# Opening of a two-block transformer kernel: squares added on VectorE into one tile, one sum on TensorE, and the spreading product two half columns later

## What is computed

```python
m  = (silu(c)     @ w_ada[l] + b_ada[l]).reshape(b, 1, N_MOD, d)      # nine modulation vectors
mc = (silu(c_ctx) @ w_ada[l] + b_ada[l]).reshape(1, 1, N_MOD, d)
x  = x + 0.5 * m[:, :, 2] * swiglu(modulate(rmsnorm(x, norm_ffn1[l]), m[:, :, 0], m[:, :, 1]), w_ffn1_in[l], w_ffn1_out[l])
# rmsnorm: x * rsqrt(mean(x * x) + EPS) * g      modulate: h * (1 + scale) + shift
```

## Time and profile before

| | before |
|---|---|
| median of 3 runs | 1579.8 us (1579.7 to 1580.3) |
| profiled execution, first to last instruction | 1577.3 us |
| TensorE matmul busy | 1418.1 us, 90% |
| VectorE busy | 1121.3 us, 71% |
| ScalarE busy | 618.1 us, 39% |
| GpSimd busy | 403.3 us, 26% |
| DMA | 435.95 MB, mean 276 GB/s |

### The profile page before, as it was taken

How to read it: one execution, slowest core, us unless ns; L and a number is a source line. 1 busy time by engine, 2 the same in 40 slices (tenths; PEclk the granted TensorE clock), 3 DMA queues, 4 the chain that set the end, 5 groups by cost and what they waited for, 6 DMA issues and landing times.

```text
span 1577.3 us, 19688 instructions
## 1 busy us (share of the span) xinstructions
PE 1418.1 (90%) x7237; PEld 1050.6 (67%) x7237; DVE 1121.3 (71%) x2287; ACT 618.1 (39%) x1353; POOL 403.3 (26%) x385
## 2 busy tenths in 40 slices
PE   8899999999999999999999998888887777777777
PEld 6688888889888999999889994333333333333322
DVE  3876775557876687777898778677777666666754
ACT  4222122213566444445565654333333333333322
POOL 0000010001200100011006236544454444444440
PEclk9999999999999999999999999999999998999999
DMA  8754585445642366555545589999999999999996
GB/s 323 272 191 143 167 287 191 159 138 171 209 147 67 121 201 187 170 176 170 160 134 163 197 330 401 420 421 422 422 421 422 420 422 421 421 422 421 422 422 282
DMA packets 86191, 435.95 MB, mean 276 GB/s; under 512 B 9488, under 2 KB 13584, under 8 KB 53072
## 3 DMA queue, kind: packets, MB, share of 16 engines
q0 software_dynamic: 45024, 298.08, 46.9%
q1 hardware_dynamic: 41072, 136.62, 26.8%
HBM read 433.61 MB, written 1.05 MB: 276 GB/s over the span
## 4 chain that ended last, share of the span: by engine, by line
PE 63%; DMA 15%; DVE 15%; ACT 4%; issue 1%; POOL 1%; SPq 0%; ACTq 0%; DVEq 0%; POOLq 0%
PE ps L585 15%; PE ps L586 15%; PE ps L587 15%; PE ps L1005 13%; DMA HF<-in_puv,AB 8%; DMA WF<-in_puv,AB 4%; DMA work<-in_puv,AB 2%; DVE WR L1411 2%; DVE work L2248 1%; PE ps L623 1%; DVE HF L2248 1%; PE ps L764 1%; ACT L1386 1%; DVE ring L2248 1%; ACT WR L1025 1%
## 5 line engine op out<-in xcount | busy, mean ns | idle before, releaser
L585 PE MATMUL ps<-HR,WR 128*128 128x256 f32 (+2 forms) x1224 | 389.1, 318 | 8.5 <-DVE WR L1411 6.9
L586 PE MATMUL ps<-HR,WR 128*128 128x256 f32 (+2 forms) x1224 | 384.4, 314 | 0.0
L587 PE MATMUL ps<-HR,WR 128*128 128x256 f32 (+2 forms) x1224 | 384.4, 314 | 0.0
L1411 DVE TENSOR_TENSOR WR<-ring,WR 128x1024 fp32r<-128x1024 f32 (+1 forms) x245 | 285.6, 1172 | 118.7 <-ACT WR L1025 117.2
L1025 ACT CAST WR<-ring 128x1024 fp32r<-128x1024 f32 (+1 forms) x245 | 241.8, 993 | 291.7 <-PE ps L587 291.6
L585 PEld LDWEIGHTS ps<-HR,WR 128*128 128x128 f32 x1224 | 233.7, 191 | 26.1 <-issue 7.3
L586 PEld LDWEIGHTS ps<-HR,WR 128*128 128x128 f32 x1224 | 233.8, 191 | 14.0 <-issue 0.2
L587 PEld LDWEIGHTS ps<-HR,WR 128*128 128x128 f32 x1224 | 233.6, 191 | 14.0
L585 PE MATMUL ps<-AR,WR 128*128 128x256 f32 (+1 forms) x535 | 165.4, 309 | 0.9 <-DVE AF L1818 0.9
L586 PE MATMUL ps<-AR,WR 128*128 128x256 f32 (+1 forms) x535 | 164.9, 308 | 0.0
L587 PE MATMUL ps<-AR,WR 128*128 128x256 f32 (+1 forms) x535 | 164.9, 308 | 0.0
(11 more groups left out here) (335 smaller groups left out, 2245.3 us busy)
## 6 DMA issues: line engine op xcount, KB each, us to landing
AB<-in_w_adaT POOLq DMA_DIRECT2D x56, 512.0 KB, 4.6
ring<-in_f1i SPq DMA_DIRECT2D x44, 512.0 KB, 4.6
ring<-in_f2i SPq DMA_DIRECT2D x44, 512.0 KB, 3.6
ring<-in_w SPq DMA_DIRECT2D x29, 512.0 KB, 3.5
ring<-in_f1o SPq DMA_DIRECT2D x21, 512.0 KB, 3.9
ring<-in_f2o SPq DMA_DIRECT2D x16, 512.0 KB, 3.6
ring<-in_wq SPq DMA_DIRECT2D x16, 512.0 KB, 4.4
ring<-in_w_ada SPq DMA_DIRECT2D x12, 512.0 KB, 9.1
```

The costliest lines, as they stand in the source:

```text
L585: e.matmul(o, l[0], r[0], start=first, stop=False)
L586: e.matmul(o, l[0], r[1], start=False, stop=False)
L587: return e.matmul(o, l[1], r[0], start=False, stop=last)
L1411: e.tensor_tensor(WS[:, m % NSP, 1, 0:nk * cols], ring[:, ring_of(m) % NS, 0:nk * cols], WS[:, m % NSP, 0, 0:nk * cols].bitcast(F32), ALU. ...
```

## The change

Three tables are written in another order, and VectorE adds more:

- VectorE adds all eight squares into `S(0)`, with seven additions in place of four; each waits for the one before it.
- TensorE makes one sum, 4 products in place of 16.
- In TensorE's order both halves of block 1 and the first half of block 2 stand ahead of the spreading product, with columns 0 and 1; before, it was the first half of block 1 and column 0.
- ScalarE copies out the rows of block 1 (`row_out(1)`) ahead of the root, and no longer behind the shift of block 0.

```diff
-OPEN = [half(0, 0), half(0, 1), ("sum", 0), ("sum", 1), ("sum", 2), ("column", 0), ("sum", 3), half(1, 0), ("spread",), half(1, 1)]
-OPEN += around(2) + around(3) + [("f1", 0, (0, 1)), ("f1", 1, (0, 1))] + around(4)
+OPEN = [half(0, 0), half(0, 1), half(1, 0), ("column", 0), half(1, 1), ("sum",), half(2, 0), ("column", 1), ("spread",), half(2, 1)]
+OPEN += around(3) + [("f1", 0, (0, 1)), ("f1", 1, (0, 1))] + around(4)
...
                 elif s[0] == "sum":
-                    p = s[1]
-                    o = bank("rms", "x") if p == 0 else bank_of("rms", "x")
-                    q.wait_ge(*dv.at("sq", "x", p))
+                    o = bank("rms", "x")
+                    q.wait_ge(*dv.at("sq", "x"))
                     for t_ in range(4):
-                        x = e.matmul(o[:, t_:t_ + 1], S(2 * p)[:, 128 * t_:128 * t_ + 128], K("ones")[:, 0:1],
-                                     start=p == t_ == 0, stop=p == t_ == 3)
-                    if p == 3:
-                        x.then_inc(*mm.to("rms", "x"))
+                        x = e.matmul(o[:, t_:t_ + 1], S(0)[:, 128 * t_:128 * t_ + 128], K("ones")[:, 0:1],
+                                     start=t_ == 0, stop=t_ == 3)
+                    x.then_inc(*mm.to("rms", "x"))
...
             row_out(0)
+            row_out(1)
             root(("x",), small[:, 0:4])
...
             column(0)
-            row_out(1)
             hi(1)
...
-            for p in range(4):
-                q.wait_ge(*ac.at("sq", "x", 2 * p + 1 if p < 3 else 6))
-                if p == 2:
+            for a, b_, last in ((0, 1, 1), (2, 3, 3), (0, 2, 3), (4, 5, 5), (0, 4, 5), (6, 7, 6), (0, 6, 6)):
+                q.wait_ge(*ac.at("sq", "x", last))
+                if b_ == 5:
                     last_square("x", XT[:, 7, :], S(7), (s_x[1], 16))
-                if p == 3:
-                    q.wait_ge(*dv.at("sqlast", "x"))
-                e.tensor_tensor(S(2 * p), S(2 * p), S(2 * p + 1), ALU.add).then_inc(*dv.to("sq", "x", p))
+                q.wait_ge(*dv.now())
+                e.tensor_tensor(S(a), S(a), S(b_), ALU.add).then_inc(*dv.to("sq", "x"))
```

## The result

The change takes 3.8 us off: median 1576.26 us (1575.16 to 1578.35, 12 runs) against 1580.04 us (1578.92 to 1581.54, 12 runs), a ratio of 0.9977 with a 95% interval of 0.9970 to 0.9985. The forecast was 1576.2. The profiled execution took 1573.3 us in place of 1577.3.

The account below looks back on a forecast made before the run. The opening was taken as one chain: TensorE to column 3, VectorE to block 7, a load, TensorE again. 3.9 won less 0.3 given back gives 3.6 us, 1576.2 against 1579.8; 8-in-10 range 1574.6 to 1579.3.

Parts of the forecast that it names:

- The start: TensorE behind block 0, which ends at 11.15 us: idles 2.25 us until block 1's weights land at 13.4.
- The additions: VectorE behind block 7's square: four dependent additions, 4 x 0.73 = 2.92 us, tile ready at 16.99, 0.3 ahead of TensorE.
- The spreading product: TensorE: 0.9 us at the upper clock level, half of 1.80; VectorE goes on at 21.4, 1.8 us earlier.
- Column 2: TensorE waits 1.5 us for ScalarE's copy of block 2's rows, does the column at 26.5; gain set here, 3.9 us.
- Behind it: From column 2 to TensorE's restart: same order, restart at 65.6 in place of 69.50 us, transfers cost nothing.
- Given back: Around TensorE's restart: the clock's rise may not move along with it; 0.3 us lost, bounds 0 to 1.95.
- Rival 1: The clock falls in TensorE's new idle time ahead of block 1; gain 1.2 us, 1578.6 us; chance 0.17.
- Rival 2: A later wait, above all TensorE's 5.49 us ahead of 69.50, takes up the gain; 1579.8 us; chance 0.10.
- Rival 3: Slower: lower clock from 13.4 us to beyond the spreading product, column 2 at 33.2; 1582.6 us; chance 0.04.
- Rival 4: Timed runs before lose two more half products to the clock than the profile; 2 x 0.8 more won, 1574.6; chance 0.09.

Follow-up runs that it names:

- after again: The changed kernel run and profiled once more with nothing altered, on one chip with another run: 1577.26 us, ratio to before 0.9979.

## Why the prediction was right

**The start.** Right. The wait for block 1's weights was 2.34 us (2.25 said); they landed 0.3 us later than in the profile before, an execution's own scatter (13.15 to 13.97 in the profiles here), and what hangs on them is that much later than written.

**The additions.** Right to 0.02: four dependent additions took 2.94 us (2.92 said), and the sum's start, 17.59, is that of TensorE and not of VectorE, whose tile was ready at 17.24. A dependent addition starts 0.73 to 0.80 us behind its predecessor; the two independent ones of before, each 0.69 long and 1.28 together, start 0.6 apart. So a link costs 0.13 us or more, and not the 0.04 of the prediction; its sum came out because it took 0.69, and not 0.6, as the step without dependence. The flush that the Trainium skill names (VectorE: DVE Perf Modes, The DRAIN you can't avoid) would have put the end at about 18.7 by the same start, an estimate; the trace does not agree, since it shows 17.24.

**The spreading product.** Mis-sized by 0.2: 1.08 us from start to start, where I had halved 1.80. With the 0.3 of the later landing VectorE went on at 21.90, 1.3 earlier than before and not 1.8.

**Column 2.** Right: 26.92, behind a wait of 1.56 us for ScalarE (1.5 said), with the gain larger here (3.5) than at the spreading product (1.3). The run with block 2's rows early shows that the wait was ScalarE's order: without it the first mark came 2.03 earlier, 0.4 of it from the landing.

**Behind it.** Right, and the strongest part: the distance from the first feed-forward product to GpSimd's loads is 26.36 us before and 26.35 after. No transfer was late: block 6's weights took 5.8 us to land in place of 7.4, and VectorE took them up at 38.45 without a wait (38.05 said).

**Given back.** The size was met by chance. In the first profile the clock rose at about 71.3 (0.68 over 70 to 72), 5.2 us behind the restart, where it was 4.5 before, and the gain went from 3.43 to 3.05 us: 0.38 lost, 0.3 said. In the second profile of the same kernel it rose at about 69.5 (0.62 over 68 to 70), 3.9 us behind its restart at 65.63, and the gain grew from 3.87 to 4.13. Over all the profiles here the rise lies 3.6 to 6.1 us behind the restart, so the term can have either sign. Behind the opening all do the same work, and yet the gain goes on moving. The table follows four VectorE instructions (lines of the kernel before) through three profiles:

| start, us | before | after | gain | after again | gain |
|---|---|---|---|---|---|
| L1582 | 93.70 | 90.65 | 3.05 | 89.57 | 4.13 |
| L1848 | 534.21 | 530.54 | 3.67 | 531.96 | 2.25 |
| L2134 | 898.36 | 894.70 | 3.66 | 896.91 | 1.45 |
| L2257, first | 1573.33 | 1569.34 | 3.99 | 1572.54 | 0.79 |

One place where the three part is 504 to 520 us, with a mean clock of 0.68, 0.89 and 0.79; another is 438 to 442 us, with 1.00, 1.00 and 0.57. The span of the first profile is 4.0 us shorter and that of the second 0.8, for the same kernel. So the opening's 3.5 us is what the change does, shown at the same two marks in both profiles (3.48 and 3.49; 3.57 and 3.56), and medians over many runs, 3.8 and 3.5 us, average over the rest. That the forecast of 3.6 lies within 0.2 of both is in part luck: the chain won 0.4 less than the 3.9 written, and the 0.3 set against it was not a loss of the change.

**The rivals.** Rival 1, the clock falling in the new wait, exists: eight profiles have this wait unfilled, with 1.15 to 2.37 us, and one of them shows the fall (three have over 2.2 us). There it took 1.6 us at the first mark, less than the 2.7 I had worked out, since the level was back before the second half product of block 1 began. The Trainium skill says (TensorE: Matmul & The Clock Gate, What's actually happening) that activity releases the throttle. The trace agrees: the clock was back at about 17.5 us, when half (1,0) had run. Rival 2, a gain lost at the gap ahead of 69.50, is out: the gap is 5.54 us, and 5.14 in the second profile, and moved with the rest. Rival 3 was not seen in any profile. Rival 4, a larger gain because the timed runs of before lose more than its profile, is not needed: 3.8 measured, 3.6 said. There is no second profile of the kernel before, so where the clock falls in its other executions is not shown.

**What the forecast had not separated.** It added up times along one path and had no shares for the parts. The runs give them, and they are not additive: the fewer products alone, -1.2 us at the first mark; the order alone, -0.8; both, +3.5. Each half of the change by itself still meets the fall of the clock (at 21.7 us in the one run, in the wait ahead of 14.01 in the other); the two together do not. In the kernel before, the higher clock is worth 3.28 us from the third sum on, and 2.25 when it is bought with a filler. The prediction prices the half products at 1.84 for 3.50 us, but says nowhere that this is most of the gain. The "two half columns" of the title are the half products (1,1) and (2,0); the second column ahead of the spreading product is worth -0.2.

## What to carry to other kernels

Fewer instructions on the busiest engine are worth nothing until the engine has other work where they stood: take the products away and move independent products into their place in one step, or neither. Where TensorE's clock falls in a stretch of thin products and waits, look at the clock before the durations, for even idle filler there can pay (2.25 us here). And follow a gain along the marks of the chain: ScalarE's in-order copy set this one at column 2, two steps behind the spreading product, and moving that copy and one weight tile was worth 1.6 us on top of the 3.5.

## What the runs showed of the hardware that was not expected

- Sixteen sum products of one column each ran back to back for 3.66 us, with no wait and with TensorE counted as fully busy, and the granted clock fell from 1.00 to 0.50 about 0.5 us behind them.
- The same list can meet the fall or not. A wait of 2.23 us was followed by a fall in one execution; waits of 2.34 and 2.37 us were not in two others, nor were five of 1.15 to 2.10 us. A wait of 1.85 us elsewhere in the list was followed by one too.
- Block 0's two half products took 5.07 to 6.47 us in the profiles with this list, against 3.65 for two at the upper level. Its first records are 0.42 us long and its last 0.27, the lengths that the records of later half products have at the lower and the upper level, although the windows show 1.00 there; where the change comes differs with the execution, and with it how long TensorE waits for block 1's weights.
- The place of the low stretches differs from execution to execution also far behind the opening: two profiles of the same kernel are 4.0 and 0.8 us shorter than the one of before. That goes with a scatter of 3 us between runs of one kernel, as large as the whole change; the marks in the opening were the sharper measure here.
